# TensorE multiplies a weight tile into an unused bank at the operand waits of the first pair of each feed-forward stage

## The reference: what is computed

```
x = x + 0.5 * swiglu(rmsnorm(x, g1), w_gate1, w_up1, w_down1)      # feed-forward 1, D_FF = 2816
h = rmsnorm(x, g); P = h @ w_in                                    # one projection, three groups of heads
x = x + concat(sliding_window(P), gated_linear(P), memory(P)) @ w_out
x = x + 0.5 * swiglu(rmsnorm(x, g2), w_gate2, w_up2, w_down2)      # feed-forward 2
swiglu(x, wg, wu, wd) = (silu(x @ wg) * (x @ wu)) @ wd
```

## Time and profile before

| | us |
|---|---|
| median of 3 runs | 1938.08 (1937.44 to 1941.73) |
| the profiled execution, its own time | 1946.86 |
| its span, first to last instruction | 1945.0 |
| matmuls busy (share of the span) | 1797.5 (92%) |
| VectorE busy | 1230.9 (63%) |
| ScalarE busy | 735.5 (38%) |
| mean granted TensorE clock | 0.968 |
| first pair of feed-forward 1, P1's start to P7's start | 22.87 to 84.06 |
| first pair of feed-forward 2, P1's start to P7's start | 1266.18 to 1320.59 |

### The profile page before, as it was taken

One profiled execution on the slowest core, in us unless ns is written; L12 is line 12 of the kernel. 1 busy time (PEld: TensorE's weight loads), 2 busy tenths in 40 slices (PEclk: granted clock), 3 DMA queues, 4 the chain that ended last, 5 costly groups with the idle time before them and its releaser, 6 DMA issues.

```text
span 1945.0 us, 24994 instructions
## 1 busy us (share of the span) xinstructions
PE 1797.5 (92%) x7798; PEld 1415.3 (73%) x7798; DVE 1230.9 (63%) x1777; ACT 735.5 (38%) x1354; POOL 539.4 (28%) x436
## 2 busy tenths in 40 slices
PE   6599999999999999999788889768999999999999
PEld 3488888888788788777344457646888888877877
DVE  7855456555596782478888864396555456548754
ACT  4533333333344641422344442134333333334433
POOL 2055345443100220001434312303454345410000
PEclk8799999999999998999899999878999999999999
DMA  6123322325934321201110111203223322385334
GB/s 166 49 93 110 122 92 86 125 101 172 341 98 130 88 81 43 76 22 36 27 29 26 29 58 65 97 1 120 92 92 118 114 92 89 125 308 187 98 87 157
DMA packets 112399, 196.54 MB, mean 101 GB/s; under 512 B 12483, under 2 KB 24948, under 8 KB 112332
## 3 DMA queue, kind: packets, MB, share of 16 engines
q1 hardware_dynamic: 111392, 194.05, 30.3%
q0 software_dynamic: 704, 1.58, 0.7%
q10 hardware_dynamic: 236, 0.06, 0.0%
HBM read 139.15 MB, written 50.33 MB: 97 GB/s over the span
## 4 chain that ended last, share of the span: by engine, by line
PE 77%; DVE 10%; DMA 5%; issue 4%; ACT 3%; SPq 1%; DVEq 0%; POOL 0%; ACTq 0%; POOLq 0%
PE ps L51 24%; PE ps L52 24%; PE ps L53 24%; DMA down_raw<-act_dram 3%; DVE A_T L1556 2%; DMA head_ones<-in_head_ones 2%; PE ps L1359 1%; ACT Pg L1482 1%; DVE gq_pad L1449 1%; PE ps L1087 1%; DVE loT L324 1%; DVE Pg L1542 1%; DVE rawT L272 1%; PE ps L1344 1%; PE ps L1352 0%
## 5 line engine op out<-in xcount | busy, mean ns | idle before, releaser
L369 DVE TENSOR_TENSOR ring<-w_raw,ring 128x512 fp32r<-128x512 f32 x264 | 253.5, 976 | 249.0 <-ACT ring L364 249.0
L51 PE MATMUL ps<-hiT,ring 128*128 128x512 f32 x704 | 279.8, 397 | 40.6 <-issue 21.7
L52 PE MATMUL ps<-loT,ring 128*128 128x512 f32 x704 | 278.3, 395 | 0.0
L53 PE MATMUL ps<-hiT,ring 128*128 128x512 f32 x704 | 277.8, 395 | 0.0
L51 PE MATMUL ps<-down_ring 128*128 128x512 f32 x616 | 243.2, 395 | 12.9 <-DVE down_ring L712 8.5
L52 PE MATMUL ps<-down_ring 128*128 128x512 f32 x616 | 241.2, 392 | 0.0
L53 PE MATMUL ps<-down_ring 128*128 128x512 f32 x616 | 240.8, 391 | 0.0
L51 PE MATMUL ps<-hiB,ring 128*128 128x512 f32 x528 | 209.4, 397 | 23.0 <-DVE loB L324 23.0
L364 ACT ACTIVATE ring<-w_raw 128x512 fp32r<-128x512 f32 x264 | 164.6, 627 | 173.6 <-PE ps L53 173.6
L712 DVE TENSOR_TENSOR down_ring<-down_raw,down_ring 128x512 fp32r<-128x512 f32 x176 | 126.7, 730 | 134.0 <-ACT down_ring L708 133.9
L52 PE MATMUL ps<-loB,ring 128*128 128x512 f32 x528 | 208.1, 394 | 0.0
(11 more groups left out here) (223 smaller groups left out, 3095.3 us busy)
## 6 DMA issues: line engine op xcount, KB each, us to landing
down_raw<-act_dram SPq DMA_DIRECT2D x154, 256.0 KB, 2.7
w_raw<-in_w_gate SPq DMA_DIRECT2D x88, 256.0 KB, 3.4
w_raw<-in_w_up SPq DMA_DIRECT2D x88, 256.0 KB, 3.4
act_dram<-actT SPq DMA_DIRECT2D x88, 256.0 KB, 2.0
wd<-in_w_down SPq DMA_DIRECT2D x88, 256.0 KB, 5.7
act_dram<-act SPq DMA_DIRECT2D x66, 256.0 KB, 2.0
p_raw<-in_w_proj SPq DMA_DIRECT2D x15, 512.0 KB, 3.5
xT<-in_x SPq DMA_DIRECT2D x8, 512.0 KB, 7.0
```

The source lines that it names most:

```text
L51: nc.tensor.matmul(out, w_hi, x_hi, start=first, stop=False, skip_group_check=resumed)
L52: nc.tensor.matmul(out, w_hi, x_lo, start=False, stop=False, skip_group_check=resumed)
L53: return nc.tensor.matmul(out, w_lo, x_hi, start=False, stop=last, skip_group_check=resumed)
L369: nc.vector.tensor_tensor(ring[:, e % RING, 1, :], op_source(e), ring[:, e % RING, 0, :].bitcast(F32), ALU.subtract).then_inc(op_ready, 1)
```

## The change

A new function multiplies the high half of ring operand e (its first 128 columns as the weight tile, all 512 as the moving operand) a given number of times into bank 5, which nobody reads. `ffn_tensor` calls it in the first pair for x == 0 before each wait for a part: 12 times before the first step of P1, 8 times before the first step of P5, and twice before each of the other 26 steps. These are 72 matmuls a stage, and 144 in all. The call stands behind the waits for `op_ready` and for the bank.

```
@@ build
-        BANK_X, BANK_Y, BANK_BIAS, BANK_NORM = (0, 2), (1, 3), 4, 6
+        BANK_X, BANK_Y, BANK_BIAS, BANK_NORM, BANK_BUSY = (0, 2), (1, 3), 4, 6, 5
...
+        def keep_busy(e, times):
+
+            op = ring[:, e % RING, 0, :]
+            for _ in range(times):
+                nc.tensor.matmul(ps[:, BANK_BUSY, :], op[:, 0:P], op, start=True, stop=True)
+
@@ ffn_tensor
                         for k in range(KK):
                             if first and x == 0:
+                                keep_busy(e, 12 if name == "P1" and k == 0 else 8 if name == "P5" and k == 0 else 2)
                                 wait(pe, part_ready, part_count(f, r, k))
```

## The result

The changed kernel takes 1951.49 us (median of 6 runs, 1950.5 to 1957.03) against 1940.07 us for the kernel before (6 runs): the ratio is 1.0057, with a 95% interval of 1.0038 to 1.0075, so +11.1 us. The forecast was +10.9 us: 1949.0 us, in a range of 1942.5 to 1955.

The account below looks back on a forecast made before the run. TensorE was taken as the bound over most of the span, VectorE's chain ahead of P7. 48 matmuls a stage at nothing and 24 at 0.226 us gave +10.9 us: 1938.1 to 1949.0 us, range 1942.5 to 1955.

Parts of the forecast that it names:

- 48 matmuls a stage ahead of P7 cost nothing: Added matmuls in P1, P2, P5 and P6 fall beside the VectorE chain that sets P7's start: taken at nothing.
- 24 a stage behind P7's start are paid at 0.226 us: Added matmuls in P7, P4 and P3 lie on TensorE's own path: 5.4 us a stage, 10.9 us for both.
- What the half clock costs at P7 does not grow: At P7 the half clock lasts a span of time, until about 89.3 us, so added matmuls do not lengthen it.
- VectorE and ScalarE do not feel it: Ahead of P7, VectorE and ScalarE do not slow down because TensorE works; the copy to G12 stays at 83.4.
- The clock rival: Clock stays full at P7, giving back 2.6 and 2.1 us: +6.2 us in all, 1944.3 us; chance 0.07.
- Nothing is taken up behind the pair loop: Waits in the down products and mixer take up none of the 10.9 us; the rival had 1938 us, chance 0.07.
- The sum against the profiled execution: Whole-kernel span of the profiled execution, 1945.0 us, plus 10.9 us gives 1955.9 us.
- The signs in the profile: P7's first product 0.5 to 0.9 us after 84.06, clock 0.50 to about 89, second-stage G12 copies 5.4 us later.

Follow-up runs that it names:

- The doubled run: The kernel before with four added matmuls in place of two before each step of P7, P4 and P3, none elsewhere: 1961.42 us, ratio 1.0098.
- the early copies: The kernel before with ScalarE's two copies for which P7 waits put ahead of its work on T4 and B22: 1933.0 us, ratio 0.9957.
- the run with early copies and matmuls in the gap: The kernel before with the two early copies and 20 matmuls of a B11 tile ahead of P7's first wait: 1934.27 us, ratio 0.9962.

## Why the prediction was right, point by point

- *48 matmuls a stage ahead of P7 cost nothing.* Shown: the run with these alone has a ratio of 0.9993 and P5 to pair 2 unchanged within 0.06 us. P6 ended about 0.8 us earlier than predicted (74.5, not 75.3, by P7's idle time of 9.87 us). The mean clock from 56.4 to 66 us was 0.81 in this execution, against 0.70 before.
- *24 a stage behind P7's start are paid at 0.226 us.* Shown: the run with these alone has the change's ratio, 1.0056, and +5.38 and +5.43 us.
- *What the half clock costs at P7 does not grow.* Right in the second stage (+5.37 in the changed kernel); in the first the half clock ended after 3.0 us and not 5.3, which gave 1.2 us back (+4.25). The run with the matmuls behind P7's start alone had +5.38, and the one with those ahead of it alone -0.03, so neither part shortens the half clock. That the two together do not either was not shown: the changed kernel has one profile.
- *VectorE and ScalarE do not feel it.* Right: VectorE's 10.72 us before P7 stayed.
- *The clock rival* did not come true, and the reason given fits: `keep_busy` stands behind `copied`. 42 matmuls a stage put ahead of the wait gave 4.6 us, which the rival had priced at 4.7. How few of them would do was not tried.
- *Nothing is taken up behind the pair loop.* The ratio of the full change and that of the part behind P7 both give the 10.9 us whole. The doubled run came out 3 us short, but the long waits there did not shrink.
- *The sum against the profiled execution* (span 1955.9) was off: the span is 1949.6. It took the 8.8 us between that execution and the median for something that the changed kernel's execution would share. It did not share them: see the last section.
- *The signs in the profile* came out in part. P7's first product was to stand at 84.6 to 85.0 and stands at 85.35, 0.3 of it from the chain; the clock from 84 to 89.3 was 0.69 and not 0.50; the second stage's copy to G12 was to come 5.4 us later and came 1.3 later (1321.24 against 1319.91). The last two go with the places where the half clock fell in the two profiled executions. So the median came out by the terms of the sum, while the trace agrees with them only stretch by stretch.

## What to carry to other kernels

Filler matmuls are free only in idle time that something else bounds, and they must stand ahead of the wait that ends the gap: behind it they come too late to hold the clock, and they delay the product that the wait was for. Before filling a gap, look at what ends it; here it was the place of a copy in ScalarE's order, worth 5.8 us a stage from P5 to pair 2, against 2.3 for the clock. And when one product gets faster, name its successor's waits first: behind the early copies, what the clock won on P7 was lost at P4 until the next copy moved too.

## What the runs showed that was not expected

**The half clock comes and goes with the execution.** In the down products of the profiled execution of before, TensorE waits 2.17 us for an add and then works at the half clock:

```profile
642.43 0.71 PE L51 MATMUL ps<-down_ring 128*128 128x512 f32 x1 [2.17 <-DVE xT L759]
642.93 0.63 PE L52 MATMUL ps<-down_ring 128*128 128x512 f32 x1
643.36 0.63 PE L53 MATMUL ps<-down_ring 128*128 128x512 f32 x1
643.79 0.63 PE L51 MATMUL ps<-down_ring 128*128 128x512 f32 x1
```

The steps are 0.43 us until 645.9, 1.6 us lost in all. In the changed kernel's trace the same place has a wait of 2.07 us, and full clock behind it. A second such spell stands at 1881.6 to 1884.5 in the trace of before and not in the changed kernel's (1.6 us), and around 743 the mean clock over 15 us is 0.78 before and 0.89 after, another 1.6 us. These three make up 4.9 us of the 6.3 by which the two spans' difference (4.6) fell short of the 10.9 forecast, and 1.2 more are the shorter half clock at P7. Single executions of the kernel before went from 1935.25 to 1948.94 us on one chip; that such spells make this spread is likely, but only single profiles show them, so it was not shown. Of the eleven traces, of whatever kernel, four have the first spell and seven the second. The spells are not all that differs between traces: in the pair loop of the first stage TensorE waits 1.18 us for ScalarE's copy in the run with the part behind P7 alone (at 480.12), 1.34 us in the run with early copies and matmuls in the gap (at 468.83), and not at all in the traces of the two kernels.

**Some of the spread lies in the start.** The first-pair chain of feed-forward 1 starts when the last constant lands, and P5's start moved between 56.5 and 57.7 us from one run's profile to the next, with no order by kernel.
